# Weighing the values for both heads of a pair at once, from four buffers of turned probabilities

## The reference, cut to what matters

```
s = einsum('bqhgd,bkhd->bhgqk', q, k) * scale        # scores
p = softmax(s)                                       # B adds a sink; A: p = p0 - lam * p1
out = einsum('bhgqk,bkhd->bqhgd', p, v)              # "weigh": probabilities times values
```

## Time and profile before

| | |
|---|---|
| time of the profiled execution | 5237.16 us |
| its span in the trace | 5235.3 us |
| median of 3 runs | 5237.1 us |
| TensorE (PE) busy | 5096.8 us, 97% |
| VectorE (DVE) busy | 3237.9 us, 62% |
| ScalarE (ACT) busy | 1682.5 us, 32% |
| GpSimd (POOL) busy | 1268.3 us, 24% |
| mean granted TensorE clock, share of full | 0.986 |

### The profile page before, as it was taken

The page is one execution under the profiler, slowest core; times in us unless marked ns, Lnnn a source line. Parts: engine busy times, 40 slices in busy tenths (PEclk is TensorE's granted clock), DMA queues, the critical chain, the costliest instruction groups (busy, mean ns, idle before and its releaser), DMA issues.

```text
span 5235.3 us, 68750 instructions
## 1 busy us (share of the span) xinstructions
PE 5096.8 (97%) x25730; PEld 4123.0 (79%) x25730; DVE 3237.9 (62%) x7229; ACT 1682.5 (32%) x2618; POOL 1268.3 (24%) x826
## 2 busy tenths in 40 slices
PE   7999999999999999999999999999999999999999
PEld 4666887788888888888876668868888888888887
DVE  3865211149899876666648652111698998666666
ACT  3344321333333332222233442213333333322222
POOL 1300221224434421111113002202344434111111
PEclk9989999999999999999999899999999999999999
DMA  7100121456787788888820001211577787888886
GB/s 281 34 26 1 48 73 60 189 206 220 264 282 253 246 310 290 290 290 290 288 76 29 26 1 55 70 60 61 205 253 242 268 280 238 319 289 289 289 290 222
DMA packets 349898, 982.01 MB, mean 188 GB/s; under 512 B 31648, under 2 KB 101408, under 8 KB 346272
## 3 DMA queue, kind: packets, MB, share of 16 engines
q1 hardware_dynamic: 216000, 553.19, 31.7%
q0 software_dynamic: 74880, 276.86, 15.3%
q10 hardware_dynamic: 58720, 148.04, 7.2%
HBM read 829.43 MB, written 148.54 MB: 187 GB/s over the span
## 4 chain that ended last, share of the span: by engine, by line
PE 85%; DVE 8%; DMA 2%; ACT 2%; issue 1%; DVEq 1%; ACTq 0%; POOL 0%; POOLq 0%; SPq 0%
PE PS L925 27%; PE PS L882 23%; PE PS L502 14%; PE PS L491 5%; PE PS L906 4%; PE PS L645 3%; PE PS L673 3%; DVE AR L1319 2%; PE PS L657 1%; PE PS L492 1%; PE PS L615 1%; DVE AR L1340 1%; DVE SM L1358 1%; DMA gates_by_expert<-AR 1%; PE PS L828 0%
## 5 line engine op out<-in xcount | busy, mean ns | idle before, releaser
L925 PE MATMUL PS<-HB,VR 128*128 128x512 f32 x6144 | 1394.8, 389 | 3.4 <-DVE HB L1619 3.4
L925 PEld LDWEIGHTS PS<-HB,VR 128*128 128x128 f32 x6144 | 1154.1, 188 | 244.9 <-issue 5.0
L882 PE MATMUL PS<-HR,UR 128*128 128x512 f32 x4128 | 1008.0, 398 | 0.0
L1662 POOL TENSOR_TENSOR UR<-WR,UR 128x1024 fp32r<-128x1024 f32 x212 | 529.5, 2499 | 1822.5 <-ACT UR L1125 945.7
L502 PE MATMUL PS<-HR,UR 128*128 128x320 f32 (+1 forms) x5952 | 914.2, 312 | 14.0 <-DVE HR L1294 9.7
L502 PEld LDWEIGHTS PS<-HR,UR 128*128 128x128 f32 x5952 | 877.3, 188 | 44.4 <-issue 27.4
L882 PEld LDWEIGHTS PS<-HR,UR 128*128 128x128 f32 x4128 | 764.3, 189 | 165.7
L1606 DVE TENSOR_TENSOR VR<-HT,VR 128x1024 fp32r<-128x1024 f32 x256 | 313.7, 1226 | 455.9 <-ACT VR L1244 368.1
L1244 ACT CAST VR<-HT 128x1024 fp32r<-128x1024 f32 x256 | 268.8, 1050 | 960.1 <-PE PS L925 955.9
L882 PE MATMUL PS<-HR 128*128 128x512 f32 x2016 | 486.6, 394 | 0.0
L882 PEld LDWEIGHTS PS<-HR 128*128 128x128 f32 x2016 | 372.1, 188 | 73.5
(11 more groups left out here) (201 smaller groups left out, 6076.4 us busy)
## 6 DMA issues: line engine op xcount, KB each, us to landing
WR<-in_uT SPq DMA_DIRECT2D x256, 512.0 KB
HT<-in_vtab SPq DMA_DIRECT2D x256, 512.0 KB, 4.6
activations<-AR ACTq DMA_DIRECT2D x256, 256.0 KB
gates_by_expert<-AR ACTq DMA_DIRECT2D x128, 512.0 KB, 3.6
HW<-activations SPq DMA_DIRECT2D x256, 256.0 KB
WR<-gates_by_expert SPq DMA_DIRECT2D x64, 1024.0 KB
AR<-in_ada SPq DMA_DIRECT2D x40, 1024.0 KB, 7.6
WR<-in_wgate SPq DMA_DIRECT2D x64, 640.0 KB, 3.9
```

Source lines behind the costliest of these rows:

```text
L882: last = pe.matmul(bank(n % 2), u_part(n, w)[:, c, :], HR[:, h, c, 0:LAT], start=c == 0 and i == 0, stop=c == DC - 1 and i == 2)
L925: last = pe.matmul(bank(d), VR[:, m % 4, w, P * d:P * d + P], HB[:, (m + 1) % 3, h, :], start=m == 0 and i == 0, stop=m == E1 - 1 and i == 2)
L1662: nc.gpsimd.tensor_tensor(dst, src, high.bitcast(F32), ALU.subtract).then_inc(sem_, 1)
```

## The change

`weigh` now takes a pair, not a unit. It runs in every second step (s = 4, 6, 8, ...), waits for the copies of both heads, and goes over the key tiles once: for each key tile, the matmul of head 0 (output partitions 0 to 63) and that of head 1 (partitions 64 to 127) follow each other. One signal stands for both heads. There are four buffers of turned probabilities, by `u % 4`, so the copy of unit u waits for the pair two before it. The buffers move out of the arena into a name of their own, `turned_probs`, which is opened and closed before `UR` is allocated and so has the place of `UR` (the split weight blocks), which isn't in use during the attention: its first block for the next stage is written by ScalarE behind its last copy of the attention.

```diff
         HT = sb("HT", [P, DC, TOK])
+        with nc.sbuf_tensor("turned_probs", [P, 4 * D], F32) as TP:
+            pass
+
         UR = sb("UR", [P, 2, 2, D], F32R)
...
         PB = t_.take(3, 2, 640)
-        PT = t_.take(2, 640)
+        PT = TP[:, 0:4 * 640].rearrange("p (a b) -> p a b", a=4)
...
-            def weigh(l, u):
-                br, j, t, hh = units[u]
-                h = 2 * j + hh
-                pe.wait_ge(pt_ready, l * NU + (u + 1))
-                if hh == 0 and u >= 4:
-                    pe.wait_ge(o_done, l * (NU // 2) + (u // 2 - 1))
-                v = {"A": lambda kt: VT[:, kt, 64 * h:64 * h + 64],
-                     "B": lambda kt: VT[:, kt, 256 + 64 * (h // 2):320 + 64 * (h // 2)],
-                     "C": lambda kt: VT[:, kt, 384 + 64 * (h // 2):448 + 64 * (h // 2)],
-                     "D": lambda kt: VD[:, kt, 64 * h:64 * h + 64]}[br]
+            def weigh(l, pair):
+                br, j, t, _ = units[2 * pair]
+                pe.wait_ge(pt_ready, l * NU + 2 * (pair + 1))
+                if pair >= 2:
+                    pe.wait_ge(o_done, l * (NU // 2) + (pair - 1))
+
+                def v(kt, hh):
+                    h = 2 * j + hh
+                    if br == "D":
+                        return VD[:, kt, 64 * h:64 * h + 64]
+                    at = {"A": 64 * h, "B": 256 + 64 * (h // 2), "C": 384 + 64 * (h // 2)}[br]
+                    return VT[:, kt, at:at + 64]
+
                 tiles = key_tiles(br, t)
-                out = PF[64 * hh:64 * hh + 64, 3072 + 512 * (u // 2 % 2):3072 + 512 * (u // 2 % 2) + P]
+                at = 3072 + 512 * (pair % 2)
                 for i, kt in enumerate(tiles):
-                    last = pe.matmul(out, v(kt), PT[:, u % 2, P * i:P * i + P], start=i == 0, stop=i == len(tiles) - 1)
-                last.then_inc(pv_done, 1)
+                    for hh in range(2):
+                        last = pe.matmul(PF[64 * hh:64 * hh + 64, at:at + P], v(kt, hh), PT[:, (2 * pair + hh) % 4, P * i:P * i + P],
+                                         start=i == 0, stop=i == len(tiles) - 1)
+                last.then_inc(pv_done, 2)
...
-                    if s >= 3:
-                        weigh(l, s - 3)
+                    if s >= 4 and s % 2 == 0:
+                        weigh(l, (s - 4) // 2)
...
-                if u >= 2:
-                    act.wait_ge(pv_done, l * NU + (u - 1))
+                if u >= 4:
+                    act.wait_ge(pv_done, l * NU + 2 * ((u - 4) // 2 + 1))
                 n = P * len(key_tiles(br, t))
-                nc.scalar.copy(PT[:, u % 2, 0:n], PF[:, 2048:2048 + n]).then_inc(pt_ready, 1)
+                nc.scalar.copy(PT[:, u % 4, 0:n], PF[:, 2048:2048 + n]).then_inc(pt_ready, 1)
```

## The result

The changed kernel takes 5279.6 us (median of 4 runs, 5266.49 to 5286.13), the kernel before 5239.26 beside it: 1.0074 times as long, 95% interval 1.0059 to 1.009. It is slower by 0.74%, where 5221 was forecast; the range ended at 5256.

A forecast was written before the change was run, and what follows sets the result against it. TensorE was taken to bound the kernel, with a ScalarE copy chain nearly as long beside it in the attentions. Gains of 7.2 (C), 4.4 (D), 3.8 (A and B) and 1 (clock), 16.4 us together, gave 5221; range 5196 to 5256.

The forecast's parts named there:

- The pass over two heads: Attention's weigh of a five-tile pair: both heads overlap and take 1.26 us, bounds 1.24 and 2.33.
- The steps: Attention, latent pairs of C and D: period 6.02 us against 6.40 and 6.12; gains 7.2 and 4.4 in all.
- The idle time of 0.8: Sign in C and D: the turn behind a weigh-free step idles about 0.8 us, waiting for ScalarE.
- Four buffers, the place, the waits: Attention's turned-probability buffers, their new place and the copy and weigh waits: each costs nothing, 56 us at most.
- The clock: Lower-clock stretches in A and B: half of the weighs falls away there, 1 us gain, bounds 0 and 4.
- The rival that had the mechanism: TensorE's new waits bring four more lower-clock stretches in C and D, costing 26 us: 5247, chance 0.12.
- The prediction's own sign of being wrong: Attention: forecast is wrong if the pass exceeds 1.5 us or a low-clock stretch stands in C or D.
- The rival without overlap: Attention's weigh: the two heads don't run beside each other, pass 2.33 us, time 5288, chance 0.10.
- The whole work saved reaches the time: Attention: all TensorE time saved in the weighs shortens the kernel, 77 us, to 5160; chance 0.04.

The follow-up runs named there:

- with fillers: Changed kernel plus one unread 384-column matmul in each step without a weigh, ahead of the turn that waits for the copy: 5218.15 us, ratio 0.9966.
- the run made for it: Changed kernel with weigh's two loops exchanged, all key tiles of head 0, then all of head 1: 5302.88 us, ratio 1.0132.
- The mixed order with filler: Changed kernel, ScalarE's copy ahead of its exponentials in B, C and D only, unread 384-column matmuls in A and B's weigh-free steps: 5181.86 us, ratio 0.9898.

## Why the prediction was wrong

*The pass over two heads*: right. 1.26 was forecast, 1.24 measured. The Trainium skill ("TensorE: Matmul & The Clock Gate", Part 3, What overlaps and what doesn't) lets weight loads run beside matmuls in flight only where the row groups differ. Here twenty loads and twenty matmuls on the same 128 rows lie in 1.07 and 1.31 us, so the trace doesn't bear the rule out for two output halves.

*The steps*: right. The period of a latent pair is 5.99 in C and in D (6.02). The second half of C in layer 0, at full clock, takes 26.7 (pairs of 4.99, 5.99, 5.56, 5.37, 4.76; forecast 26.8), the first half of D with fillers 26.4 and 26.7 (forecast 26.6). Three things were off by little. The idle time of 0.8 had been worked out for C, where it is 0.93; in D, where the turn comes sooner behind the scores, it is 1.27. The second half of C took 28.3 before, not the 28.6 that the sum used for all. And the last half of D ends with the phase and gains nearly nothing (21.8 for 21.9), so D gives 0.7 and 0.4 in a layer with fillers, not 2.2; C with fillers gives 2.9 and 3.2 of 3.6.

The change's own gain, by halves and stages at full clock: in C 26.5 for 28.6 and 26.7 for 28.3, in D 26.1 and 26.4 for 27.7 and 0.15 in the last half, none of them with filler; in B 50.3 (with filler) for 51.2. A has no such pair of windows; by its pairs at full clock, of the kernel before and of the changed one with filler, it gains 0.3 to 1. For two layers that is an estimate of 13 to 15 us, where 15.4 was forecast without the clock.

*Four buffers, the place, the waits*: right at nothing, shown by the run with them alone.

*The clock*: this step failed. The text put 1 us of gain on it, and under the rivals gave as the reason against a lower clock that "the same products are computed in about the same time, only more densely". The time at the lower level rose from 63 to 216 us in the two attentions; at 0.32 us each that is 49 us. Against a gain of 13 to 15 this gives some 35 of loss, where the attentions show 31. The rival that had the mechanism, with its price of 0.33, was given 0.12 and four stretches in C and D, 26 us. What the runs showed in its place: the clock falls in all four stages. Half of the added low time is in B (0.82 to 0.55 in layer 0), which was partly at the lower level before and where the rival put none; C and D have 59 us of it, some 19 us of time. With a filler in the holes the clock and 30 us of each attention are back. The prediction's own sign of being wrong, a low stretch in C or D, is there. The prediction had both facts in hand: that the clock falls at holes in the trace of before, and that its own sum opens a hole in every second step. In the forecast it priced the second by the wait alone.

*The rival without overlap* named 5288 and the mechanism; the run made for it was 5303, of which the pass was less than priced and the clock the rest.

*The whole work saved reaches the time*, 5160, needs a chain without the copy behind the exponential. The mixed order with filler, at 5182, went a good part of that way; some 17 of its 57 us are the clock's (54 us fewer at the lower level than before, at 0.32), the rest is saved work. The prediction saw that chain as what takes the gain, and in C and D it was.

What stays open: what it is in TensorE's work that the clock answers to. The filler runs tell what works here and what doesn't, and the run with the heads one after the other that their overlap isn't needed for the fall; idle time and amount of work were not separated.

## What to carry to other kernels

Before work is taken from a TensorE that bounds a stage, ask what it does in the time freed. If the next thing in its order waits for another engine, the gain becomes a hole, and if the trace of before shows the lower clock at such holes, price that for every stage with them: a microsecond at the lower level cost 0.32 here. Take the work away, close the wait where the order of another engine allows it (here ScalarE's copy, chosen by stage), and fill the holes that are left. All three together gave 5182. The shorter pass with filler gave 5218; the shorter pass with the closed wait but without filler 5234, no faster than before; the filler alone gained nothing on the kernel before, and the shorter pass alone lost.

## What the runs showed of the hardware

- Two matmul streams on output partitions 0 to 63 and 64 to 127, on the same 128 rows, run side by side in full: 20 records in 1.31 us where 10 took 1.31 us before, weight loads of 64 columns included (1.07 against 1.06).
- They seem to do so in part even without being interleaved: ten records of one half followed by ten of the other took 1.95 us until the next kind of matmul, where twenty in a row would take 2.33 by an estimate from their distance of 0.109 and 0.15 for the change of kind.
- The granted clock of a busy kernel (TensorE 97% busy on the page of the profile) stayed at 1.2 GHz for nearly all of a stage of 65 us, B of layer 0, with the matmuls busy for 59.07 of its 65.23 us; the turn's weight loads waited there 12 times for the copy, 14.6 us in all and at most 1.6 at once. One matmul of 384 columns in every second step (0.65 us from its start to that of the next turn) brought 2.4 GHz back; one of 128 columns did not (B at 0.52).
